# A four-mixer block on one core of Trainium2: nine places in the order of work, and GpSimd rounding weights

## The chip, the cores and the metric

The kernel runs on one core of a Trainium2 chip. The metric is the device time in microseconds (us) of one execution. The kernel's inputs lie in HBM; all of its work, from loading them to the last store, counts.

## The reference

The reference takes x (512 tokens, width 1024), a context of 256 tokens and a conditioning vector c through a chain of blocks, all in fp32:

```
first block, twice (L0: 512 + 256 context tokens, L1: 512 tokens; L1's context only gives keys and values):
  shift, scale, gate = split(silu(c) @ w_ada + b_ada)            # and the same of c_ctx for the context
  h = rms_norm(x, norm_g) * (1 + scale) + shift
  a_glu, a_gate, nq, nk, nv, n_gate, wq, wk, wv, w_gate, merge = split(h @ w_in)
  y_a = (silu(layer_norm(conv31(a_glu[:512] * sigmoid(a_glu[512:])))) * silu(a_gate)) @ w_proj_a
  y_b = (neighbourhood_attention(rms(nq), rms(nk), nv) * silu(n_gate)) @ w_proj_b    # 8 heads, 8 x 16 window + context, bias
  y_c = (window_attention(rope(rms(wq)), rope(rms(wk)), wv, sink) * silu(w_gate)) @ w_proj_c
  x = x + gate * ((sigmoid(g_a) * y_a + sigmoid(g_b) * y_b + sigmoid(g_c) * y_c) @ w_o)
then x + rglru_mixer(rmsnorm(x)), x + ffn(...), x + nsa_mixer(...), x + ffn(...), and a last norm
rglru_mixer: y, x = split(x @ lru_in);  xc = causal_conv4(x);  r, i = sigmoid(xc @ gate_w);
  log_a = -8 * r * softplus(-a_param);  h = scan(exp(log_a), sqrt(-expm1(2 log_a)) * i * xc);  (h * gelu(y)) @ lru_out
```

## The kernel before

Every product is made of three matmuls of fp32r operands: a weight and an activation are each split into a rounded part (WH; Hh, Gh, XH) and a remainder (WL; Hl, Gl, XL), and hi*hi, hi*lo and lo*hi are added in PSUM. Activations lie with their features on the partitions, so that a chunk of weights, 128 outputs by 1024 inputs (8 blocks of 128 x 128), is used by 24 matmuls over 512 columns, and 24 more over 256 where the context's tokens are there.

**Weights.** All chunks are numbered in the order of their use, W[0], W[1], ... SyncE loads chunk j into one of three buffers RAW (`sp_loads`), once the remainder of chunk j-3 is made. ScalarE rounds it into WH (`act_split`, L1027), when TensorE is through with the chunk three before it. VectorE subtracts for WL (`dve_split`, L1037). TensorE waits for WL (`pe_linear`, L1066, and in the branches L1585). `ahead(name)` is the chunk two after the named one: while TensorE works on one, the split of the one two later is issued. For the 32 pieces of the modulation of L1, which are woven into L0, GpSimd subtracts (`pool_split`, L1045). The last entry of a chunk in the plan says how it is split.

**The first block.** `mix(L)` runs the convolution's linears (chunks cb and ca in turn), the neighbourhood branch (br 0), the window branch (br 1) and w_o. Each branch's order of work is one list, written by `branch(L, br)`, and each engine's program walks through that list and issues its own part of each unit. A unit ("lin", name, k, ...) is block k of a chunk, three products for all columns. Phase ph has the chunks of ak, aq, av (keys, queries, values) of head pair ph and ag, mg (gates) of the pair before it. `chain` says at which linear after a chunk's begin its norm is made (nrm1, nrm2, nrm3: squares, sums over the head through TensorE, the scaling); "out" are the copies of queries and keys into QA, QB, KA, KB, shared among ScalarE, VectorE (L1985) and GpSimd (L2049); "vt" and "vout" turn the values and copy them to V (L1905). `heads(p)` gives the units of head pair p, woven between the linears of the phase after it: "st" are scores, with their exponentials Pa and Pb by ScalarE (L1787), "pv" products with V (L1708), "max" the score tiles whose maxima VectorE takes for the next head (L1655, L1661 on TensorE, L1996 on VectorE), "tr" their transposes (L1625), "fin" and "sink" the end. An integer in that list is a linear before which the next unit may not stand: 2 at the start, 22 (19 in br 1) for the next head's maxima.

`taps` are the 31 taps of the depthwise convolution, VectorE's multiply-adds (L1455), two in a unit. In L0 one unit stands after every third linear of the phases and after every second one of the branch's tail; in L1 after every fifth and every second.

The tail of br 0 has the chunks mg (1024 wide) and pj (512 wide) in turn, then cg, cm and pa. `beside` puts one tick of the modulation (a chunk of w_ada times c, L1398) after each of 32 blocks of L0's tail, and behind each eight of them a "modend", which turns the row of results into columns (L1250). A third of w_ada for L1 (part c = 3) is used at the transition from L0 to L1, in `mix(1)`, eight ticks ahead of the norm of L1.

**The recurrent mixer.** After its norm, `recur(m)` runs for ten m in a software pipeline: chunk rx of lru_in, a causal convolution of four taps (L2382, L2386), remainder (L2389), chunk gw of gate_w (256 wide), the gates. Then ten chunks ry with the scans (L2416). The splits are ScalarE's and VectorE's, as everywhere; GpSimd has nothing to do.

## Time and profile before

| | |
|---|---|
| time, median of 3 runs | 3355.71 us (3349.92 to 3362.6) |
| the profiled execution, its time | 3353.82 us |
| its span in the profile | 3352.0 us |
| mean granted clock of TensorE | 0.967 |
| busy: TensorE, VectorE, ScalarE, GpSimd | 93%, 55%, 39%, 8% |
| from HBM | 247 MB, 74 GB/s over the span |

The profile is one execution. Busy time of TensorE counts its matmuls, whose ends are modelled; the granted clock is the share of its full clock (2.4 GHz; the lower level is 1.2 GHz), and a mean between the two is a mix in time. "Waits" sum the idle time ahead of an instruction by the instruction that ended it; "issue" there is idle time whose end no shown semaphore explains. Several waits of one instruction are put down to the one that came last. L1708 is line 1708 of the kernel.

### The profile page before, as it was taken

How to read it: one execution, taken by the hardware profiler on the slowest of the kernel's cores; microseconds unless marked ns; L12 is line 12 of the kernel's file. 1: busy time of each engine (PE TensorE's matmuls, PEld its weight loads, DVE VectorE, ACT ScalarE, POOL GpSimd, SP SyncE). 2: the span in 40 equal slices, each digit the busy share in tenths (PEclk: the TensorE clock that was granted, in tenths of full speed). 3: DMA queues.
4: the chain of work that ended last, by engine and by line, in shares of the span. 5: the costliest groups of instructions: out<-in, count | busy, mean ns of one | idle time of the engine just before them, and what ended most of it. 6: DMA issues, size and time to landing. Idle time of an engine off the chain costs nothing.

```text
span 3352.0 us, 36714 instructions
## 1 busy us (share of the span) xinstructions
PE 3124.0 (93%) x14684; PEld 2439.8 (73%) x14684; DVE 1849.6 (55%) x2910; ACT 1319.7 (39%) x2028; POOL 267.8 (8%) x198
## 2 busy tenths in 40 slices
PE   8998889999999889899889998999999989999998
PEld 4876777877788567677667676788877766788876
DVE  5876675454434667674443576566525662366622
ACT  3244434234432344533444356322224556422221
POOL 0011131210000001100000000000002210000000
PEclk9999989999999899999989999999999999999999
DMA  5221122320011322123101222333332210132331
GB/s 199 70 71 57 48 82 90 109 83 26 19 38 59 105 82 82 51 82 102 32 29 44 72 88 73 98 95 94 95 91 88 91 58 1 57 100 89 98 92 61
DMA packets 78729, 251.48 MB, mean 75 GB/s; under 512 B 9120, under 2 KB 11168, under 8 KB 78560
## 3 DMA queue, kind: packets, MB, share of 16 engines
q1 hardware_dynamic: 72672, 227.91, 22.1%
q0 software_dynamic: 5024, 18.09, 1.7%
q8 instruction: 116, 1.90, 0.2%
q10 hardware_dynamic: 864, 3.15, 0.2%
q14 instruction: 53, 0.43, 0.0%
HBM read 247.01 MB, written 2.10 MB: 74 GB/s over the span
## 4 chain that ended last, share of the span: by engine, by line
PE 41%; DVE 6%; ACT 5%; issue 1%; DMA 0%; DVEq 0%; ACTq 0%; SPq 0%
PE PS L1066 29%; PE PS L1585 2%; PE PS L2521 2%; PE PS L2622 1%; PE PS L1708 1%; PE PS L1090 1%; ACT WH L1027 1%; PE PS L2599 1%; DVE U L2386 1%; PE PS L2600 1%; DVE WL L1037 0%; PE PS L2581 0%; PE PS L2543 0%; DVE IG L2416 0%; ACT PS L2675 0%
## 5 line engine op out<-in xcount | busy, mean ns | idle before, releaser
L1037 DVE TENSOR_TENSOR WL<-RAW,WH 128x1024 fp32r<-128x1024 f32 (+3 forms) x386 | 451.7, 1171 | 581.5 <-ACT WH L1027 580.6
L1027 ACT ACTIVATE WH<-RAW 128x1024 fp32r<-128x1024 f32 (+4 forms) x439 | 422.7, 967 | 475.6 <-PE PS L1066 362.5
L1585 PE MATMUL PS<-Hh,WH 128*128 128x512 f32 x1376 | 533.8, 388 | 12.1 <-DVE T L1956 7.1
L1585 PE MATMUL PS<-Hl,WH 128*128 128x512 f32 x1376 | 496.3, 361 | 0.0
L1585 PE MATMUL PS<-Hh,WL 128*128 128x512 f32 x1376 | 494.6, 359 | 0.0
L1066 PE MATMUL PS<-XH,WH 128*128 128x512 f32 x928 | 372.6, 401 | 23.1 <-DVE WL L1037 16.1
L1066 PE MATMUL PS<-XL,WH 128*128 128x512 f32 x928 | 369.3, 398 | 0.0
L1066 PE MATMUL PS<-XH,WL 128*128 128x512 f32 x928 | 369.0, 398 | 0.0
L1585 PEld LDWEIGHTS PS<-Hh,WH 128*128 128x128 f32 x1376 | 267.7, 195 | 77.7 <-issue 24.6
L1585 PEld LDWEIGHTS PS<-Hl,WH 128*128 128x128 f32 x1376 | 267.5, 194 | 49.7 <-issue 11.2
L1585 PEld LDWEIGHTS PS<-Hh,WL 128*128 128x128 f32 x1376 | 266.5, 194 | 40.3
L1455 DVE SCALAR_TENSOR_TENSOR C<-AP,SMA,C 128x512 f32<-128x512 f32 x360 | 235.1, 710 | 0.4
L1066 PEld LDWEIGHTS PS<-XH,WH 128*128 128x128 f32 x928 | 175.7, 189 | 73.1 <-ACT U L2308 11.9
L1066 PEld LDWEIGHTS PS<-XH,WL 128*128 128x128 f32 x928 | 175.7, 189 | 43.3
L1066 PEld LDWEIGHTS PS<-XL,WH 128*128 128x128 f32 x928 | 175.8, 189 | 43.0 <-issue 1.0
L1045 POOL TENSOR_TENSOR WL<-RAW,WH 128x1024 fp32r<-128x1024 f32 (+1 forms) x53 | 121.8, 2299 | 1028.3 <-ACT WH L1027 1028.3
L1066 PE MATMUL PS<-FGh,WH 128*128 128x512 f32 x384 | 156.5, 408 | 0.0
L1066 PE MATMUL PS<-Hh,WH 128*128 128x512 f32 (+1 forms) x384 | 144.8, 377 | 12.2 <-DVE WL L1037 6.9
L1066 PE MATMUL PS<-FGh,WL 128*128 128x512 f32 x384 | 151.7, 395 | 0.0
L1066 PE MATMUL PS<-FGl,WH 128*128 128x512 f32 x384 | 151.6, 395 | 0.0
L1066 PE MATMUL PS<-Hl,WH 128*128 128x512 f32 (+1 forms) x384 | 139.5, 363 | 0.0
L1066 PE MATMUL PS<-Hh,WL 128*128 128x512 f32 (+1 forms) x384 | 139.0, 362 | 0.0
(375 smaller groups left out, 5434.3 us busy)
## 6 DMA issues: line engine op xcount, KB each, us to landing
RAW<-in_w_in SPq DMA_DIRECT2D x124, 512.0 KB, 3.6
RAW<-in_ffn_in SPq DMA_DIRECT2D x96, 512.0 KB, 3.6
RAW<-in_ffn_out SPq DMA_DIRECT2D x48, 512.0 KB, 3.5
RAW<-in_w_ada SPq DMA_DIRECT2D x32, 384.0 KB, 3.6
RAW<-in_nsa_in SPq DMA_DIRECT2D x21, 512.0 KB, 3.3
RAW<-in_lru_in SPq DMA_DIRECT2D x20, 512.0 KB, 3.6
MW<-in_w_ada SPq DMA_DIRECT2D x32, 256.0 KB, 9.1
BS<-in_bs POOLq DMA_DIRECT2D x16, 512.0 KB, 3.9
```

The costliest lines, as they stand in the source:

```text
L1027: act.activation(WH[half[j]][:, 0:n], RAW[j % NRAW][:, 0:n], ACT.Copy).then_inc(*did("act_whi", ("whi", j)))
L1037: dve.tensor_tensor(WL[half[j]][:, 0:n], RAW[j % NRAW][:, 0:n], WH[half[j]][:, 0:n].bitcast(F32), ALU.subtract).then_inc(*did("dve_wlo", ( ...
L1045: pool.tensor_tensor(WL[half[j]][:, 0:n], RAW[j % NRAW][:, 0:n], WH[half[j]][:, 0:n].bitcast(F32), ALU.subtract).then_inc(*did("pool_wlo", ...
L1066: mm = pe.matmul(ps[:, c:c + n], wt[:, 128 * i:128 * i + 128], x[:, a:a + n], start=(seen == 0 and q == 0), stop=(seen == total - 1 and q ...
L1090: pe.matmul(ps[:, c:c + n], ones, b[:, a0:a0 + n], start=(k == 0), stop=(k == 7)).then_inc(*did("pe_sq", ("sqm", sq, k)))
L1455: dve.scalar_tensor_tensor(dst, src, wt, dst, ALU.mult, ALU.add).then_inc(*did("dve_tap", ("tap", L, m, k, a0), ("tap", L, m, k)))
L1585: mm = pe.matmul(ps[:, c:c + w_], wt[:, 128 * k:128 * k + 128], x[:, a:a + w_], start=(k == 0 and q == 0), stop=(k == n - 1 and q == 2))
L1708: mm = pe.matmul(dst, VV[L, br][:, b, 64 * g:64 * g + 128], src, start=first, stop=end)
L2386: dve.scalar_tensor_tensor(xc, pa[:, k:k + S], smc(cw + 4 * m + k, cw + 4 * m + k + 1), xc, ALU.mult, ALU.add).then_inc(*did("dve_c", *([( ...
L2521: mm = pe.matmul(ps[:, 0:S], wt[half[j]][:, 128 * k:128 * k + 128], x[:, k, :], start=(k == 0 and q == 0), stop=(k == 7 and q == 2))
L2599: pe.matmul(ps3, NKH[b][:, g, 128 * kt:128 * kt + 128], by_tile(NQ[:, 4 * g:4 * g + 4, :], qt), start=True, stop=False)
L2600: mm = pe.matmul(ps3, NKL[b][:, g, 128 * kt:128 * kt + 128], by_tile(Q2[g % 2], qt), start=False, stop=kt < qt)
```

## The change

The weights' splits in the attention branches are issued at unit k = 3 of a chunk instead of k = 0 by ScalarE and VectorE. A fourth way to split, POOLED, lets GpSimd both round and subtract; it is used for the chunks ak, aq, av, ag and the first mg of L1's window branch and for lru_in and gate_w. GpSimd's copies of QB and KA in L1's window branch go to ScalarE. Norms' second part moves from linear 10 to 11, third part in br 0 from 13 to 14. In br 0 head pairs start at linear 4, the next maxima at 27 (L0) or 25 (L1), and the first half of the copies at 24. Taps begin later in each phase but the first, and come every 1.8 linears in the tails. The modulation's ticks stand two blocks later and modend one block more; at the transition two of the eight ticks and the order of chunks move behind the first linear. The first norm's split of weights stands after row 2 instead of 5.

```diff
+POOLED = 4
@@ mix(L)
-            for k in range(8):
+            for k in range(4):
                 self.tick(3, k)
@@ conv(L)
             self.win(("cb", L, m), L, 512 + 128 * m)
+            if (L, m) == (1, 0):
+                for k in range(4, 8):
+                    self.tick(3, k)
@@ chain
-            c = {8: [("nrm1", nm)], 10: [("nrm2", nm)], 13: [("nrm3", nm)]}
+            c = {8: [("nrm1", nm)], 11: [("nrm2", nm)], 13 if br else 14: [("nrm3", nm)]}
@@ heads
-            start = [5] + tops(0, 0) + a + rows(0, 0) + b if p == 0 else [2]
-            ready = 19 if br else 22
+            start = [5] + tops(0, 0) + a + rows(0, 0) + b if p == 0 else [2 if br else 4]
+            ready = 19 if br else 27 if L == 0 else 25
@@ tapped
-        def tapped(units, every):
-            out, n = [], 0
+        def tapped(units, every, late=False):
+            out, n = [], -every if late else 0
...
-                    if n % every == 0 and taps:
+                    if n > 0 and int(n / every) > int((n - 1) / every) and taps:
@@ phases
-                    at.setdefault(1 if f else 18 if br else 22, []).extend(to)
+                    at.setdefault(1 if f else 18 if br else 24, []).extend(to)
-            order += tapped(made, 3 if L == 0 else 5) + ...
+            order += tapped(made, 3 if L == 0 else 5, ph > 0) + ...
-        ticks = iter(range(32 if L == 0 and not br else 0))
+        spots = iter(range(-2, 30))
         def beside(steps):
...
+            out = list(steps)
+            if L == 0 and not br and (i := next(spots)) >= 0:
+                out += tick(i)
+            return out
+        def tick(i):
+            return ([("modend", L, i // 8 - 2)] if i % 8 == 1 and i > 8 else []) + [("tick", i // 8 - 1, i % 8)]
-        order += tapped(tail, 2) + taps
+        order += tapped(tail, 1.8) + taps
-        return order + ([("modend", L, 2)] if L == 0 else [])
+        return order + (tick(30) + tick(31) + [("modend", L, 2)] if L == 0 else [])
@@ attn
+                    woven = nm[0] in ("ak", "aq", "av", "ag") or nm[0] == "mg" and nm[3] < 3 + br
+                    self.linear(nm, [((u[3], u[4], 0, 128 * u[5], POOLED if woven and L and br else 1), list(range(u[5])))])
@@ recur, lru
+        self.linear(nm, [(("lru_in", 10 + m, 0, 1024, POOLED), list(range(8)))])
+        self.chunk(("gw", m), 0, ("gate_w", m, 0, 256, POOLED))
+            self.linear(nm, [(("lru_in", m, 0, 1024, POOLED), list(range(8)))])
@@ act_split
-                if how:
+                if how and how != POOLED:
+        def pool_weights(pool, upto):
+            while done["pool"] <= min(upto, len(P.W) - 1):
+                j = done["pool"]
+                n, how = P.W[j][3:5]
+                if how == POOLED:
+                    for w in due("pool", ("raw", j), earlier[j], ("turn", done["turn"])):
+                        pool.wait_ge(*w)
+                    pool.tensor_copy(WH[half[j]][:, 0:n], RAW[j % NRAW][:, 0:n]).then_inc(*did("pool_whi", ("whi", j)))
+                    pool_split(pool, [j])
+                done["pool"] += 1
@@ act_begin (dve_begin alike)
-            act_rms(act, "in", HH[0], ..., (5, 1))
+            act_rms(act, "in", HH[0], ..., (2, 1))
@@ pe_conv
+                if (L, m) == (1, 0):
+                    for k in (6, 7):
+                        pe_tick(pe, 3, k)
@@ act_attn (dve_attn alike)
-                    if u[2] == 0:
+                    if u[2] == 3:
                         act_split(act, ahead(nm))
@@ act_out
+            if L and br:
+                if kind == "ak":
+                    to = to if f == 0 else [(KA[L, br][64:128, 1, 0:n], 64, "p1")] + to
+                else:
+                    to = to + [(QB[L, br][0:64, 0, 0:n], 0, "p0")] if f == 0 else [(QB[L, br][64:128, 1, 0:n], 64, "p1")] + to
@@ pool_attn
+            pool_weights(pool, P.wj[("ak", L, br, 0), 0] + 1)
...
-                if u[0] == "out":
+                if u[0] == "lin":
+                    if u[2] == 0:
+                        pool_weights(pool, ahead(nm))
+                elif u[0] == "out" and not (L and br):
@@ pe_mix
-                for k in range(1, 8):
+                for k in range(1, 6):
                     pe_tick(pe, 3, k)
@@ act_mix (dve_mix alike, with dve_split)
                 act_rms(act, sq, HH[L], ..., (1, P.wj[("cb", 1, 0), 0] + 1))
+                act_split(act, P.wj[("ca", 1, 0), 0])
@@ pool program
             pool_mix(pool, 1)
+            pool_weights(pool, P.wj[("ry", 9), 0])
             pool_nsa(pool)
```

## Rows read from the trace of the kernel before

**Rows 1.** Page, part 1: busy time, share of the span and instructions by engine.

```profile
...
PE 3124.0 (93%) x14684; PEld 2439.8 (73%) x14684; DVE 1849.6 (55%) x2910; ACT 1319.7 (39%) x2028; POOL 267.8 (8%) x198
...
```

**Rows 2.** Waits of PE: line <- releaser: us in total, times, longest us.

```profile
...
PE PS L1066 <- DVE WL L1037: 23.0, 11, 4.8
...
PE PS L1708 <- ACT Pa L1787: 18.2, 14, 3.0
...
PE PS L1708 <- DVE V L1905: 13.2, 6, 4.1
PE PS L1655 <- DVE QA L1985: 12.5, 4, 5.1
...
PE PS L1655 <- issue: 9.5, 4, 2.4
...
PE PS L1398 <- POOL WL L1045: 6.8, 1, 6.8
...
PE PS L1250 <- ACT T L1263: 6.0, 2, 4.8
...
```

**Rows 3.** Busy by stretch: PE, PEld, DVE, ACT, POOL (count), granted clock, DMA share.

```profile
...
223.00:295.00 72.00, 60.25 (x309) 49.60 (x307) 49.31 (x78) 29.51 (x45) 10.79 (x11) 0.93 0.20 59
430.00:470.00 40.00, 33.20 (x157) 26.89 (x158) 28.55 (x43) 12.03 (x15) 17.55 (x4) 0.81 0.30 92
1420.00:1465.00 45.00, 38.45 (x148) 29.33 (x149) 43.03 (x61) 15.05 (x20) 0.73 (x1) 0.92 0.20 54
1932.00:1990.00 58.00, 53.99 (x216) 41.91 (x216) 45.63 (x77) 27.87 (x46) 0.00 (x0) 0.94 0.25 75
1990.00:2067.00 77.00, 61.49 (x246) 47.95 (x246) 59.78 (x77) 61.03 (x81) 0.00 (x0) 0.96 0.25 73
...
```

**Rows 4.** Timeline, PE, two linears in a row at full clock: first product of each.

```profile
...
450.05 0.39 PE L1585 MATMUL PS<-Hh,WH 128*128 128x512 f32 x1
...
451.10 0.39 PE L1585 MATMUL PS<-Hh,WH 128*128 128x512 f32 x1
...
```

**Rows 5.** Timeline, PE, three stretches: start, us, instruction, idle before and its end.

```profile
...
49.77 0.80 PE L1066 MATMUL PS<-Hh,WH 128*128 128x512 f32 x1 [3.62 <-DVE WL L1037]
...
299.07 2.05 PE L1708 MATMUL PS<-Pa,V 128*128 128x512 f32 x2 [4.06 <-DVE V L1905]
...
1114.84 0.80 PE L1066 MATMUL PS<-Hh,WH 128*128 128x512 f32 x1 [3.25 <-DVE WL L1037]
...
```

**Rows 6.** Timeline, DVE, two stretches: before a copy of V, and beside POOL's splits.

```profile
...
296.78 1.15 DVE L1455 SCALAR_TENSOR_TENSOR C<-AP,SMA,C 128x512 f32<-128x512 f32 x2
...
458.25 2.58 DVE L1037 TENSOR_TENSOR WL<-RAW,WH 128x1024 fp32r<-128x1024 f32 x1 [6.79 <-ACT WH L1027]
460.76 4.37 DVE L1455 SCALAR_TENSOR_TENSOR C<-AP,SMA,C 128x512 f32<-128x512 f32 x4
...
```

**Rows 7.** Timeline, DVE, one group of the recurrent mixer (rx and gw).

```profile
...
1942.62 1.22 DVE L1037 TENSOR_TENSOR WL<-RAW,WH 128x1024 fp32r<-128x1024 f32 x1
...
1948.30 0.42 DVE L1037 TENSOR_TENSOR WL<-RAW,WH 128x256 fp32r<-128x256 f32 x1
...
1950.16 1.22 DVE L1037 TENSOR_TENSOR WL<-RAW,WH 128x1024 fp32r<-128x1024 f32 x1
```

**Rows 8.** Timeline, POOL, two stretches: its first splits and two later ones.

```profile
...
432.98 12.75 POOL L1045 TENSOR_TENSOR WL<-RAW,WH 128x1024 fp32r<-128x1024 f32 x2 [6.11 <-ACT WH L1027]
...
457.35 2.40 POOL L1045 TENSOR_TENSOR WL<-RAW,WH 128x1024 fp32r<-128x1024 f32 x1 [11.62 <-ACT WH L1027]
461.79 2.40 POOL L1045 TENSOR_TENSOR WL<-RAW,WH 128x1024 fp32r<-128x1024 f32 x1 [2.04 <-ACT WH L1027]
```

**Rows 9.** Timeline, ACT, L1's window attention: a split ahead of copies and exponential.

```profile
...
1771.07 1.06 ACT L1027 ACTIVATE WH<-RAW 128x1024 fp32r<-128x1024 f32 x1
...
```

**Rows 10.** Groups of POOL's instructions by line and shape, whole span.

```profile
...
L2049 POOL CAST QB<-T 64x768 fp32r<-64x768 f32 x16 | 17.1, 1066 | 175.0 <-DVE T L1974 136.7 <-DVE T L1964 37.5 <-POOL O L2067 0.5
...
L2485 POOL CAST Q<-NQ 64x2048 fp32r<-64x2048 f32 x3 | 5.7, 1898 | 72.1 <-PE PS L2622 72.1
...
```

More of the change, by code:

```diff
@@ L459, in branch @@
                 elif to and (ph > 1 or f == 0):
-                    at.setdefault(1 if f else 18 if br else 22, []).extend(to)
+                    at.setdefault(1 if f else 18 if br else 24, []).extend(to)
             made, late = woven(steps, at, 0, n, heads(ph - 1))
-            order += tapped(made, 3 if L == 0 else 5) + ([("gate", L, br, ph - 1, f) for f in range(2)] if ph else [])
+            order += tapped(made, 3 if L == 0 else 5, ph > 0) + ([("gate", L, br, ph - 1, f) for f in range(2)] if ph else [])
         assert not late
         order += [("split", ("ag", L, br, m)) for m in range(4)]
-        ticks = iter(range(32 if L == 0 and not br else 0))
+        spots = iter(range(-2, 30))
         def beside(steps):
-            out = steps[0:3]
-            if (i := next(ticks, None)) is not None:
-                if i and i % 8 == 0:
-                    out += [("modend", L, i // 8 - 2)]
-                steps = steps + [("tick", i // 8 - 1, i % 8)]
-            return out + steps[3:]
+            out = list(steps)
[4 more added lines that the diff above has]
+            return ([("modend", L, i // 8 - 2)] if i % 8 == 1 and i > 8 else []) + [("tick", i // 8 - 1, i % 8)]
         def merge(m):
@@ L520, in attn @@
                 if u[2] == 0:
-                    self.linear(nm, [((u[3], u[4], 0, 128 * u[5], 1), list(range(u[5])))])
+                    woven = nm[0] in ("ak", "aq", "av", "ag") or nm[0] == "mg" and nm[3] < 3 + br
+                    self.linear(nm, [((u[3], u[4], 0, 128 * u[5], POOLED if woven and L and br else 1), list(range(u[5])))])
             elif kind == "nrm1":
@@ L637, in recur @@
         nm = ("rx", m)
-        self.linear(nm, [(("lru_in", 10 + m, 0, 1024, 1), list(range(8)))])
+        self.linear(nm, [(("lru_in", 10 + m, 0, 1024, POOLED), list(range(8)))])
         self.tmp.take((nm, "pa"))
@@ L664, in lru @@
             nm = ("ry", m)
-            self.linear(nm, [(("lru_in", m, 0, 1024, 1), list(range(8)))])
+            self.linear(nm, [(("lru_in", m, 0, 1024, POOLED), list(range(8)))])
             if m in (0, 1, 3, 5, 7):
@@ L1336, in dve_begin @@
             dve_turn0(dve, 1)
-            dve_rms(dve, "in", HH[0], HL[0], [("roots",)] + [("x", i) for i in range(6)], lambda k, q: AB[:, k, q:q + 1], lambda k, q: MODS[0][:, k, q:q + 1], (5, 1))
+            dve_rms(dve, "in", HH[0], HL[0], [("roots",)] + [("x", i) for i in range(6)], lambda k, q: AB[:, k, q:q + 1], lambda k, q: MODS[0][:, k, q:q + 1], (2, 1))
         B1 = MODS[0][:, 8:16, 0]
@@ L2045, in pool_attn @@
                     for dst, at, key in to:
-                        for w in due("pool", (nm, "y2") if br else (nm, "y"), scores_read(L, br, p - 1, f), ("pool", L, br, turn)):
+                        for w in due("pool", (nm, "y2") if br else (nm, "y"), scores_read(L, br, p - 1, f), ("turn", done["turn"])):
                             pool.wait_ge(*w)
-                        turn += 1
-                        pool.tensor_copy(dst, y[at:at + 64, 0:n]).then_inc(*did("pool_st", (nm, key), (nm, "out", f), ("pool", L, br, turn)))
+                        done["turn"] += 1
+                        pool.tensor_copy(dst, y[at:at + 64, 0:n]).then_inc(*did("pool_st", (nm, key), (nm, "out", f), ("turn", done["turn"])))
                 elif u[0] == "tick":
```

24 lines of the change are left out of this document (12 added, 12 removed).

## The prediction

> **What bounds the kernel now.** The page comes first. TensorE is busy for 3124.0 us, 93% of the span of 3352.0 [rows 1]. So there are some 228 us in which it stands, plus what it loses at its lower clock, and nothing else can be won: no matmul is removed. VectorE (55%), ScalarE (39%) and GpSimd (8%) have room on average, but that says nothing of one stretch. The list of TensorE's waits is the second view, since the change is a list of stops: it names the instruction that waited, who released it, and how often [rows 2]. The stretches are the third. In 1420:1465, the tail of L1's neighbourhood branch, VectorE is busy 43.03 of 45 us and bounds the work; in the recurrent mixer (1932:1990 and 1990:2067) it is busy 79% and 78%; elsewhere it has air [rows 3]. The granted clock there is the third thing to see. With levels of 1.2 and 2.4 GHz a mean of 0.93 over 72 us means 10.1 us at the lower one, and TensorE, busy 0.84 of the time, lost 10.1 x 0.84 / 2 = 4.2 us. A linear (three products, 768 columns) takes 1.05 us at the full clock, a chunk eight of them, 8.4 us [rows 4].
>
> The sum is made against the profiled execution, 3353.8 us, 1.9 below the median of the runs, 3355.7. A run can tell a change from none at about 0.5%, 17 us.
>
> **Neighbourhood branches: heads, pins, values, copies, splits at k = 3.** The stops for QA (12.5 us, 4 times) and for V (13.2 us, 6 times) [rows 2] are waits for VectorE's copies while TensorE's next instruction is a score or a product of the other head. The longest for V, 4.06 us, is typical [rows 5]: two taps, 1.15 us, ran at 296.78 [rows 6] while TensorE stood. The heads of later phases start two linears later, the maxima wait until unit 27 instead of 22, and the split of 1.22 us [rows 7] no longer stands in front of the copies at a chunk's start. Two linears later is 2.1 us more for each wait, and the split gone is 1.2: 3.3 us against mean waits of 3.1 and 2.2. I take 20 of 25.7 us. The second rotation of norms later by one linear helps one wait and hurts the next: nothing, with 0 to +6 as bounds, as its copies are now later by the same 1.05. Of the low clock behind these stops I take 5 us (a bit over one such stretch of 4.2 us, of some four). Bounds for the part: -8 and -36. Sum -25.
>
> **The first tick of the modulation.** TensorE stood 6.8 us for GpSimd's remainder [rows 2]. That split and the next took 12.75 us together, while a later one took 2.40 [rows 8], so the first took about 10.3. Whether this was VectorE's queue of taps or the first use, no row says. With the tick two blocks later, TensorE has a chunk more of linears; if the 10.3 us come again, 1 to 2 us of waiting are left. The stretch 430:470 is granted 0.81, thus 15.2 us low, 6.3 us lost over two stops [rows 3]; I take 2.5. Sum -7.3, bounds -9.5 and -2.
>
> **Ends of the modulation one block later.** They cost 6.0 us in two waits for ACT's T [rows 2], and the clock behind, some 2. The block inserted takes more than the longest wait, 4.8. Against it two PSUM pairs of the modulation stay taken for one block, so linears have two of four: +1.5. Sum -6.5, bounds -8 and +3.
>
> **Start and transition.** The first linear waited 3.62 us for WL at 49.77, the transition's 3.25 us at 1114.84 [rows 5]. The split at k = 2 costs rows 3 to 7 of the norm about 2.1 us, and these have slack until the linear reaches them: -3. At the transition the raw chunk arrives earlier, since ticks 6 and 7 stand behind it; they still cost their own time: -2. Bounds of both: -7 and +3.
>
> **Splits off ScalarE's way.** TensorE waited 18.2 us for Pa in 14 places and 9.5 us in four places where a copy of QA by ScalarE stood last ("issue") [rows 2]. In L1's window attention ScalarE does a split of 1.06 us right before these copies and exponentials [rows 9], and L0's are alike. Moving it to k = 3 or to GpSimd could take 1.06 from each of 18 waits, 19 us; a wait of mean 1.3 us is often shorter than that, and half of the time something else is next. L1's second branch pays one more copy of about 0.6 us on ScalarE per half. Sum -9, bounds -19 and 0.
>
> **L1's tail.** VectorE bounds it, and it gets 26 taps instead of 22, and its splits later in the chunk, where TensorE needs them sooner. A tap is 0.58 to 0.74 us (1.15 for two) [rows 6]: 4 x 0.73 = 2.9, and about as much for late remainders: +6, bounds +2 and +9. In L0's tail VectorE is busy 28.55 of 40 us [rows 3], which covers four more taps.
>
> **GpSimd splits the recurrent mixer.** No row shows GpSimd rounding a 128x1024 chunk. Its casts of 64x768 take 1.07 us and of 64x2048 1.90 us [rows 10], so about 1.2 for 1024; with the subtraction of 2.40 [rows 8] a chunk costs 3.6 us, a chunk of 256 about 1.3, against 1.22 and 0.42 on VectorE [rows 7]. The price lies in the two engines together: VectorE's remainder that began at 458.25 lasted 2.58 instead of 1.22 us and ended 1.08 us after GpSimd's subtraction, which ran 457.35 to 459.75; the four taps at 460.76 lasted 4.37 instead of 2.3, with GpSimd's at 461.79 inside [rows 6, 8]. So I count their work there as one queue. The group rx and gw takes 7.54 us now, from 1942.62 to 1950.16 [rows 7], and VectorE is busy 0.79 of it [rows 3], 5.93; without 1.22 and 0.42 that is 4.29. With GpSimd's 4.9 it is 9.2 us, 1.65 more per group, 16.5 over ten. For the ten ry chunks VectorE has 59.78 - 12.2 = 47.6 us, GpSimd 36: 83.6 against a stretch of 77 [rows 3]: +6.6. Sum +23. The ends: without any such lock all waits of L1066 for WL but the two priced above go (23.0 - 3.6 - 3.3 = 16.1 us) and some 4 us of clock, -20; with delays inside VectorE's chain of dependent instructions, and with GpSimd's first chunks running against the norm ahead, +38.
>
> The Trainium skill ("SBUF — State Buffer", section "Who interferes with whom") says that the pair of ports that the two engines share is an exclusive lock for a whole instruction, and that a VectorE instruction with at most one SBUF input is free of it; of the group's instructions the two tensor-scalar ones (about 1.05 us, by the length of two taps) would then be outside, the group 8.15 us, and the mixer's price some +12 instead of +23. The trace agrees with the lock in the two places above; that a one-input instruction escapes it, no row of mine shows.
>
> **GpSimd splits L1's window attention.** VectorE is idle for most of this stretch, so it meets GpSimd less: +2 for longer copies, bounds -3 and +10.
>
> **Sum:** -25 - 7.3 - 6.5 - 5 - 9 + 6 + 23 + 2 = -21.8. That is 3332 for the profiled execution and 3334 against the median.
>
> **Rivals.**
> A, the forecast, 3334 us, chance 0.42; its own spread is 15 us each way, so that it can fall within 0.5%.
> B, the two engines hardly disturb each other in the mixer. For it: the subtraction itself stays at 2.40 us beside busy taps [rows 8], and GpSimd does nothing at all in the mixer now [rows 3]. Against it: the 2.58 us. The mixer gives -20, the time is 3334 - 43 = 3291. Chance 0.20.
> C, the stops move. The matmuls stay as many, and a wait taken from V or QA comes back at the next product, for Pa, Pb or a transpose, because the heads' chain of scores, exponentials and products is itself what is late. For it: Pa already is the wait with the most places, 14 [rows 2]. Against it: the longest waits end with a copy that stood behind other work. Then some 33 of the 53 us won outside the mixer are kept, and mixer, tail and window attention cost 31: 3355.7 - 2 = 3354. Chance 0.21.
> D, slower: one mechanism, the mixer's weights on GpSimd. If its two instructions for a chunk take 5 us instead of 3.6 because they wait for VectorE's as well, VectorE's 4.3 and GpSimd's 7 stand in one line and the group takes 11 us, 3.5 more; ten groups cost 35 and the ry chunks 15. With 8 for the tail and window attention and 33 won elsewhere that is 3355.7 + 25 = 3381. It decides from about 10.5 us per group on, where the mixer eats all that the rest gains (30 + 15 = 45 = 53 - 8). For it: the first split of 10.3 us beside VectorE's taps [rows 8]. Against it: the later ones at 2.40. Chance 0.17.
>
> **How the numbers follow.** Faster by over 0.5% is below 3338.9: most of B, six tenths of A, a tenth of C: 0.19 + 0.25 + 0.02, and a little for sizes that I took low: 0.49. Slower, above 3372.5: most of D and a little of C: 0.19. The rest, 0.32, is within 0.5%. The range from 3290 to 3373 leaves out a third of B and two thirds of D. That is A's own 3319 to 3349 widened by B and C.
>
> **What would show it.** In the changed trace: no wait of TensorE over 1.5 us for V and QA in L0's neighbourhood branch, and a clock of 0.96 or more there; the first tick's wait under 2 us; none over 1 us for ACT's T at the modulation's ends. GpSimd's subtraction at 2.40 us but its rounding spread widely; VectorE's three-operand instructions in the mixer at mean over 1.0 us instead of about 0.75; the spacing of rx chunks 9 us instead of 7.54; TensorE's clock falling there. In L1's tail 6 us more. The prediction is wrong in its main point if the mixer's groups keep 7.5 us or less, or if the waits for V and QA come back under other names with the same total.

## The result: 0.8% slower, and the profile after

The changed kernel takes 3385.1 us (median of four runs, 3380.5 to 5035.7) against 3355.5 for the one before (four runs, 3349.9 to 3362.6): ratio 1.0083, interval 1.0057 to 1.0108. In a later comparison five runs of it took 3380.0 to 3381.6 us, and the ratio is 1.0067 (1.0053 to 1.0080). The run of 5035.7 us had a mean granted clock of 0.554 and is left out of the ratio; the profile shown here is of another execution of the same kernel, 3378.2 us in span. The first view is the page, as in [rows 1].

```profile
span 3378.2 us, 36730 instructions
...
PE 3121.0 (92%) x14684; PEld 2438.2 (72%) x14684; DVE 1866.2 (55%) x2866; ACT 1290.6 (38%) x1993; POOL 403.0 (12%) x277
...
```

TensorE does the same 14684 matmuls and is busy as long as before; it stands some 29 us more. GpSimd's busy time went from 267.8 to 403.0 us. VectorE's rose from 1849.6 to 1866.2 although it makes 44 remainders fewer, some 46 us of work: its other instructions became longer. What TensorE waits for, in the columns of [rows 2] (L1608 is the old L1585, L1086 the old L1066, L1731 the old L1708, L1678 the old L1655, L1648 the old L1625, L1653 the old L1630, L1270 the old L1250):

```profile
...
PE PS L1608 <- DVE T L1984: 20.4, 8, 3.3
PE PS L1086 <- ACT U L2341: 20.1, 3, 10.7
PE PS L1731 <- ACT Pa L1810: 17.6, 15, 4.1
PE PS L1653 <- DVE T L1992: 17.0, 6, 4.0
PE PS L1678 <- DVE QA L2013: 16.8, 5, 6.9
...
PE PS L1086 <- DVE XL L1161: 13.4, 4, 12.6
PE PS L1608 <- DVE WL L1045: 12.9, 7, 4.1
PE PS L1678 <- issue: 11.6, 4, 5.0
...
PE PS L1648 <- ACT T L1833: 9.2, 6, 1.9
...
PE PS L1270 <- ACT T L1283: 2.1, 1, 2.1
...
```

The 13.2 us for V are gone, those for ACT's T of the transposes (L1648) fell from 19.8 to 9.2, and the first tick's 6.8 us are gone. In their place stand the waits for T of the norms, 20.4 and 17.0 us (7.1 and 3.2 before, at the old L1585 and L1630), and those of the mixer, for ACT's U and for XL. QA was 12.5 us in four places and is 16.8 in five. In L0's neighbourhood phases alone (120 to 431 us) no wait of TensorE for V or QA is left under its name, where there were 9.5 and 10.1 us; but T of the norms went from 2.4 to 10.4 us, "issue" ahead of the score tiles from nothing to 9.9, and TensorE's waits there add up to about 41 us, as before. Then the stretches, as in [rows 3]:

```profile
...
430.00:470.00 40.00, 38.36 (x211) 31.85 (x211) 39.20 (x58) 10.49 (x13) 15.18 (x4) 0.99 0.41 117
1930.00:1990.00 60.00, 52.53 (x220) 40.58 (x219) 51.65 (x55) 15.00 (x25) 39.38 (x30) 1.00 0.25 71
1990.00:2020.00 30.00, 17.69 (x61) 13.36 (x60) 24.21 (x29) 14.20 (x22) 13.00 (x9) 0.77 0.29 87
...
```

The first tick's stretch (430:470), 0.81 before, is now granted 0.99 and TensorE is busy 38.36 of 40 us in it. The mixer's clock falls to 0.77 in 1990:2020, behind two stops of 6 us.

The traces were laid side by side by the start of the same matmul in both (the one of each chunk's first 512 columns with WL), which gives how much longer each stage became. The second column is the changed kernel, the third the same with the mixer's weights back on ScalarE and VectorE (e1_lru_back), the fourth that one with the branches' splits back at unit 0 (f3_split_k0); us against before, of one execution each:

| stage | changed | mixer back | and splits at 0 | forecast |
|---|---|---|---|---|
| start and L0's convolution | -4.2 | -4.1 | -3.5 | -3 |
| L0, neighbourhood phases | -0.1 | +2.0 | -13.1 | most of -25 |
| first tick | -10.3 | -10.3 | -10.6 | -7.3 |
| rest of L0's tail | +11.5 | +11.5 | +7.8 | -6.5 |
| L0, window attention | +9.6 | +9.7 | +5.5 | most of -9 |
| w_o and transition | -2.3 | -2.4 | -3.5 | -2 |
| L1, neighbourhood phases | +8.4 | +8.4 | -0.6 | rest of -25 |
| L1's tail | +5.3 | +5.3 | +5.2 | +6 |
| L1, window attention | -18.5 | -18.5 | -14.0 | +2 |
| mixer | +27.5 | +0.3 | +0.3 | +23 |

Behind the mixer none of the experiments below changes anything, and still the profiled executions of all these kernels lie there between 1.2 us below and 5.8 us above that of the kernel before. A single stage of a single execution is thus no firmer than a few us.

### The profile page after: what moved, and what is told of

Its sections match the earlier page's. It is cut to its first block, busy times and chain, and to the rows that moved or that the text cites. A ratio compares the mean times of both kernels' runs of the same rounds, so it can differ in the third digit from the quotient of the medians.

```text
span 5033.8 us, 36730 instructions
## 1 busy us (share of the span) xinstructions
PE 4957.0 (98%) x14684; PEld 2993.4 (59%) x14684; DVE 1872.7 (37%) x2866; ACT 1299.6 (26%) x1993; POOL 386.7 (8%) x277
## 4 chain that ended last, share of the span: by engine, by line
PE 52%; DVE 1%; ACT 1%; issue 0%; DMA 0%; ACTq 0%; DVEq 0%; SPq 0%
PE PS L1086 35%; PE PS L2554 4%; PE PS L1608 4%; PE PS L2655 1%; PE PS L1110 1%; PE PS L1731 1%; PE PS L2632 1%; PE PS L2614 1%; PE PS L2633 1%; PE PS L2615 1%; PE PS L2576 0%; PE PS L2323 0%; PE PS L1741 0%; PE PS L2648 0%; PE PS L2637 0%; PE PS L1711 0%
## 5 line engine op out<-in xcount | busy, mean ns | idle before, releaser
L1608 PE MATMUL PS<-Hh,WH 128*128 128x512 f32 x1376 | 743.6, 540 | 1.0 <-DVE WL L1045 0.6
L1045 DVE TENSOR_TENSOR WL<-RAW,WH 128x1024 fp32r<-128x1024 f32 (+2 forms) x342 | 396.9, 1161 | 833.5 <-ACT WH L1035 832.4
L1608 PE MATMUL PS<-Hh,WL 128*128 128x512 f32 x1376 | 696.2, 506 | 0.0
L1608 PE MATMUL PS<-Hl,WH 128*128 128x512 f32 x1376 | 696.1, 506 | 0.0
L1035 ACT ACTIVATE WH<-RAW 128x1024 fp32r<-128x1024 f32 (+3 forms) x395 | 383.7, 974 | 853.8 <-PE PS L1086 658.7
L1086 PE MATMUL PS<-XH,WH 128*128 128x512 f32 x928 | 537.8, 580 | 12.2 <-DVE XL L1161 12.2
L1086 PE MATMUL PS<-XL,WH 128*128 128x512 f32 x928 | 535.2, 577 | 0.0
L1086 PE MATMUL PS<-XH,WL 128*128 128x512 f32 x928 | 534.9, 576 | 0.0
L1608 PEld LDWEIGHTS PS<-Hh,WH 128*128 128x128 f32 x1376 | 314.8, 229 | 179.7 <-issue 115.1
L1608 PEld LDWEIGHTS PS<-Hl,WH 128*128 128x128 f32 x1376 | 320.2, 233 | 159.0 <-issue 101.2
L1608 PEld LDWEIGHTS PS<-Hh,WL 128*128 128x128 f32 x1376 | 311.1, 226 | 126.0 <-issue 51.2
L1054 POOL TENSOR_TENSOR WL<-RAW,WH 128x1024 fp32r<-128x1024 f32 (+2 forms) x97 | 211.1, 2176 | 1309.6 <-ACT WH L1035 1306.1
L1086 PEld LDWEIGHTS PS<-XH,WH 128*128 128x128 f32 x928 | 202.8, 219 | 169.8 <-issue 104.6
L1086 PEld LDWEIGHTS PS<-XL,WH 128*128 128x128 f32 x928 | 203.5, 219 | 154.6 <-issue 92.7
L1086 PEld LDWEIGHTS PS<-XH,WL 128*128 128x128 f32 x928 | 203.4, 219 | 152.8 <-issue 89.1
L1086 PE MATMUL PS<-FGh,WH 128*128 128x512 f32 x384 | 229.9, 599 | 0.0
L1086 PE MATMUL PS<-FGh,WL 128*128 128x512 f32 x384 | 221.3, 576 | 0.0
L1086 PE MATMUL PS<-FGl,WH 128*128 128x512 f32 x384 | 220.9, 575 | 0.0
L1086 PE MATMUL PS<-Hh,WH 128*128 128x512 f32 (+1 forms) x384 | 203.3, 529 | 2.4 <-DVE Hl L1163 2.4
L1086 PE MATMUL PS<-Hh,WL 128*128 128x512 f32 (+1 forms) x384 | 197.0, 513 | 0.0
L1086 PE MATMUL PS<-Hl,WH 128*128 128x512 f32 (+1 forms) x384 | 196.2, 511 | 0.0
```

The costliest lines, as they stand in the source:

```text
L1035: act.activation(WH[half[j]][:, 0:n], RAW[j % NRAW][:, 0:n], ACT.Copy).then_inc(*did("act_whi", ("whi", j)))
L1045: dve.tensor_tensor(WL[half[j]][:, 0:n], RAW[j % NRAW][:, 0:n], WH[half[j]][:, 0:n].bitcast(F32), ALU.subtract).then_inc(*did("dve_wlo", ( ...
L1054: pool.tensor_tensor(WL[half[j]][:, 0:n], RAW[j % NRAW][:, 0:n], WH[half[j]][:, 0:n].bitcast(F32), ALU.subtract).then_inc(*did("pool_wlo", ...
L1086: mm = pe.matmul(ps[:, c:c + n], wt[:, 128 * i:128 * i + 128], x[:, a:a + n], start=(seen == 0 and q == 0), stop=(seen == total - 1 and q ...
L1608: mm = pe.matmul(ps[:, c:c + w_], wt[:, 128 * k:128 * k + 128], x[:, a:a + w_], start=(k == 0 and q == 0), stop=(k == n - 1 and q == 2))
```

## Experiments

Medians in us, with the difference from the kernel before, which ran on the same chip beside each group (e, f, g, h: 3358.2, 3356.1, 3357.1, 3357.1 us), and the ratio to it with its 95% interval. The four groups ran on four chips, so kernels of different groups are compared by the third column: what an edit wins or costs is the difference of two of its entries. The expectations compare bare medians, which gives up to 2 us more or less.

| kernel | median | against before | ratio, interval |
|---|---|---|---|
| changed (e0_after) | 3380.4 | +22.2 | 1.0067, 1.0053 to 1.0080 |
| mixer's weights back (e1_lru_back) | 3358.1 | -0.1 | 0.9998, 0.9989 to 1.0007 |
| window attention's back (e2_wa_back) | 3400.0 | +41.8 | 1.0124, 1.0110 to 1.0138 |
| both back (e3_both_back) | 3373.5 | +15.3 | 1.0047, 1.0034 to 1.0060 |
| e1 and norms as before (f1_norms_back) | 3363.0 | +7.0 | 1.0020, 1.0010 to 1.0031 |
| e1 and heads as before (f2_heads_back) | 3360.7 | +4.7 | 1.0014, 1.0005 to 1.0024 |
| e1 and splits at unit 0 (f3_split_k0) | 3330.1 | -26.0 | 0.9923, 0.9908 to 0.9938 |
| e1 and taps as before (f4_taps_back) | 3349.7 | -6.4 | 0.9984, 0.9975 to 0.9994 |
| f3 and taps as before (g1_k0_taps) | 3331.2 | -26.0 | 0.9931, 0.9914 to 0.9947 |
| f3 and norms as before (g2_k0_norms) | 3325.5 | -31.6 | 0.9908, 0.9893 to 0.9922 |
| f3 and heads as before (g3_k0_heads) | 3338.2 | -18.9 | 0.9947, 0.9932 to 0.9962 |
| f3 and window attention's weights back (g4_k0_wa) | 3344.3 | -12.9 | 0.9963, 0.9950 to 0.9976 |
| e1, only ScalarE's split at unit 0 (h2_act0) | 3329.3 | -27.8 | 0.9917, 0.9902 to 0.9931 |
| g2, the ry chunks on GpSimd (h3_ry_pool) | 3333.6 | -23.5 | 0.9930, 0.9915 to 0.9945 |
| g2, first copies at 22 (h4_out22) | 3320.1 | -37.0 | 0.9890, 0.9875 to 0.9905 |
| h4, L1's taps every second linear (h5_out22_taps) | 3312.6 | -44.5 | 0.9866, 0.9850 to 0.9883 |

**The changed kernel as it is.**

> The changed kernel as it is, for a profile at the full clock and a time beside the next three. Both theories: 3380 to 3386 us. Theory one (the mixer): the recurrent mixer, from its norm to its last ry chunk, is 40 us or more longer than before and the rest of the kernel 10 to 25 us shorter. Theory two (the places): the mixer is at most 15 us longer and the rest 15 us or more longer, its stops having moved.

The time fits both theories, and the stages fit neither: the mixer is 27.5 us longer, between the 40 of the one and the 15 of the other, and the rest is neither shorter nor longer.

**The mixer's weights back.**

```diff
-        self.linear(nm, [(("lru_in", 10 + m, 0, 1024, POOLED), list(range(8)))])
+        self.linear(nm, [(("lru_in", 10 + m, 0, 1024, 1), list(range(8)))])
...
```

> The changed kernel with lru_in's and gate_w's chunks split by ScalarE and VectorE again, all else as changed. Theory one (the mixer's weights on GpSimd cost 40 to 60 us): 3330 to 3345 us, faster than the kernel before. Theory two (the price lies in the moved places or the window attention): 3370 us or more. My forecast's own price for this edit, 23 us, would give 3362.

It wins 22.3 us, the price that the forecast had. It ends at the time of the kernel before, outside both theories (3330 to 3345, and 3370 or more) and nearest to the forecast's own price, 3362. Everything else together was worth nothing.

**The window attention's weights back, and both.**

```diff
-                    self.linear(nm, [((u[3], u[4], 0, 128 * u[5], POOLED if woven and L and br else 1), list(range(u[5])))])
+                    self.linear(nm, [((u[3], u[4], 0, 128 * u[5], 1), list(range(u[5])))])
```

> The changed kernel with the weights of L1's window attention split by ScalarE and VectorE again (at unit 3 of a chunk), the copies of QB and KA still ScalarE's, the mixer still GpSimd's. Theory one: within 6 us of the changed kernel, 3379 to 3391. Theory three (the window attention's weights on GpSimd are what costs, their 3.6 us a chunk being too long for a chunk of 5.6 us with the copies between): 3360 us or less.

> Both edits undone: no weights rounded by GpSimd at all. Theory one: as with the mixer's alone undone, 3325 to 3345 us, so the moved places by themselves win 10 to 30 us. Theory two: 3365 us or more, the moved places lose by themselves.

No theory had this: without GpSimd's splits in the window attention the kernel is 19.6 us slower (15.4 between e1 and e3), and in the trace the difference lies in that stage: -18.4 us against before in e0, +1.5 in e2. What is left without any rounding by GpSimd, the moved places alone, loses 15 us, as theory two had it.

**One place at a time, from e1.**

```diff
# f1: norms
-            c = {8: [("nrm1", nm)], 11: [("nrm2", nm)], 13 if br else 14: [("nrm3", nm)]}
+            c = {8: [("nrm1", nm)], 10: [("nrm2", nm)], 13: [("nrm3", nm)]}
# f2: heads, pins, copies
-            start = [5] + tops(0, 0) + a + rows(0, 0) + b if p == 0 else [2 if br else 4]
-            ready = 19 if br else 27 if L == 0 else 25
+            start = [5] + tops(0, 0) + a + rows(0, 0) + b if p == 0 else [2]
+            ready = 19 if br else 22
-                    at.setdefault(1 if f else 18 if br else 24, []).extend(to)
+                    at.setdefault(1 if f else 18 if br else 22, []).extend(to)
# f3: splits, in ScalarE's and in VectorE's program
-                    if u[2] == 3:
+                    if u[2] == 0:
# f4: taps
-            order += tapped(made, 3 if L == 0 else 5, ph > 0) + ...
-        order += tapped(tail, 1.8) + taps
+            order += tapped(made, 3 if L == 0 else 5) + ...
+        order += tapped(tail, 2) + taps
```

> From the changed kernel with the mixer's weights back on ScalarE and VectorE (3358 us): the norms' second part at linear 10 again instead of 11, and the third at 13 in both branches. Theory P (the later norms cost, since the chunk after waits for the PSUM pair that the third part reads, and the rotation waits for the third part): the waits for T at L1984 and L1992, 20.4 and 17.0 us, fall to about 7 and 3, the waits for T at L1833 rise by about 10, and the time is 3335 to 3348 us. Rival Q (the places are neutral one by one, a chain of exponentials and products is what is late): 3352 us or more, the waits only change their names.

> From the same kernel: heads of later phases of the neighbourhood branch start at linear 2 again, next maxima at 22, first copies at 22. Theory P: the heads' later start won the V stops but lengthened the stops for QA; taking it back brings V's 13 us back and takes as much from QA and Pb: 3350 to 3366 us, no clear change. My forecast's view (the later heads win 20 us): 3375 us or more. A view in which they lose by themselves: 3345 us or less.

> From the same kernel: ScalarE and VectorE split the weights of the attention branches at unit 0 of a chunk again instead of unit 3. Theory P (splits at unit 3 fall onto the norm's work, which now comes one linear later): 3345 to 3355 us, mostly in L1's tail (some 3 us) and in the T waits. My forecast's view (unit 3 frees copies and exponentials, worth up to 19 us): 3365 us or more.

> From the same kernel: taps as before (no late start in the phases, one unit after every second linear of the tails, 22 instead of 26 units in L1's tail). Theory P: L1's tail wins back 3 to 5 us of its 5.3, L0's phases lose less than that: 3352 to 3358 us. Rival (late taps are what makes room for copies of QA and V): 3362 us or more.

The splits at unit 3 cost 25.9 us, more than any view had. Norms: theory P fell, the later ones win 7 us here. Heads: 4.7 us won, as P had it; the intervals of e1 and f2 overlap. By stage the later heads win 8.0 us in L0's phases and lose 8.6 in L1's. Taps: 6.3 us lost, a little more than P had. So the late split is the largest single part of what the forecast missed. The trace shows how. Unit 3 of a chunk is linear 11 counted from the begin of the chunk before, and there the norm's second part stands. Three timelines of the changed kernel (start, us, engine, line, operation, idle before): ScalarE, VectorE, and the linear of TensorE that waits:

```profile
...
247.75 1.05 ACT L1839 ACTIVATE T<-PS,EPSC 128x384 f32<-128x384 f32 x2 [2.54 <-PE PS L1648]
248.69 0.94 ACT L1843 ACTIVATE T<-T 128x384 f32<-128x384 f32 x2
249.52 1.05 ACT L1035 ACTIVATE WH<-RAW 128x1024 fp32r<-128x1024 f32 x1
...
```

```profile
...
250.60 1.23 DVE L1045 TENSOR_TENSOR WL<-RAW,WH 128x1024 fp32r<-128x1024 f32 x1 [1.76 <-ACT WH L1035]
251.75 1.14 DVE L1478 SCALAR_TENSOR_TENSOR C<-AP,SMA,C 128x512 f32<-128x512 f32 x2
252.81 0.68 DVE L2031 TENSOR_REDUCE STAT<-PS 128x2 f32<-128x512 f32 x1
253.52 0.97 DVE L2045 TENSOR_TENSOR PS<-PS,O 64x768 f32<-64x768 f32 x1
...
256.40 1.01 DVE L1980 SCALAR_TENSOR_TENSOR T<-T 128x384 f32<-128x384 f32 x2
257.33 1.01 DVE L1984 SCALAR_TENSOR_TENSOR T<-PS,T 128x384 f32<-128x384 f32 x2
...
```

```profile
...
258.40 0.50 PE L1608 MATMUL PS<-Hh,WH 128*128 128x512 f32 x1 [3.34 <-DVE T L1984]
...
```

ScalarE makes the norm's logarithms and exponentials (to 249.6) and then rounds the weight, to 250.57. VectorE's queue has the subtraction at the same place, so it stands 1.76 us idle for WH, then subtracts. Only then come two taps, a reduction and the three instructions that end a head, none of which needs the weight, and the norm's third part at 256.40, 6.8 us after the exponentials. The linear at 258.40 waits for that part's second step (L1984), because it needs the PSUM pair that the step reads: 3.34 us. In the kernel with splits at unit 0 the same stretch, VectorE and then ScalarE:

```profile
...
238.06 1.23 DVE L1045 TENSOR_TENSOR WL<-RAW,WH 128x1024 fp32r<-128x1024 f32 x1 [1.61 <-ACT WH L1035]
...
245.25 0.97 DVE L2045 TENSOR_TENSOR PS<-PS,O 64x768 f32<-64x768 f32 x1 [0.43 <-ACT O L1894]
...
248.13 1.01 DVE L1980 SCALAR_TENSOR_TENSOR T<-T 128x384 f32<-128x384 f32 x2
...
```

```profile
...
236.98 1.05 ACT L1035 ACTIVATE WH<-RAW 128x1024 fp32r<-128x1024 f32 x1
...
242.57 0.94 ACT L1843 ACTIVATE T<-T 128x384 f32<-128x384 f32 x2
...
```

Rounding and subtraction are over at 239.3, ahead of the norm's logarithms. The exponentials end at 243.5 and the third part starts at 248.13, 4.6 us later instead of 6.8. TensorE's waits in that kernel, whole span, in the same columns:

```profile
...
PE PS L1731 <- ACT Pa L1810: 22.0, 14, 4.1
...
PE PS L1648 <- ACT T L1833: 11.1, 8, 2.3
...
PE PS L1608 <- DVE T L1984: 7.0, 5, 2.2
...
PE PS L1653 <- DVE T L1992: 7.0, 6, 2.8
...
```

T of the norms fell from 20.4 to 7.0 and from 17.0 to 7.0.

**Which engine's late split.**

```diff
# ScalarE's program only
-                    if u[2] == 3:
+                    if u[2] == 0:
                         act_split(act, ahead(nm))
```

> From the changed kernel with the mixer's weights back (3358 us): in the attention branches ScalarE rounds at unit 0 again, VectorE subtracts at unit 3. If VectorE's wait for WH in front of the norm's third part is what the late split costs (its idle time, 1.8 us, at 250.6 in the trace), most of the 28 us come back: 3332 to 3340 us. If VectorE's own 1.2 us at that place, and WL coming late, are what costs: 3346 to 3356 us.

All of it comes back, 27.7 us, with VectorE's subtraction still at unit 3. The same stretch of this kernel, ScalarE and then VectorE:

```profile
...
235.36 1.05 ACT L1035 ACTIVATE WH<-RAW 128x1024 fp32r<-128x1024 f32 x1
...
240.95 0.94 ACT L1843 ACTIVATE T<-T 128x384 f32<-128x384 f32 x2
...
```

```profile
...
240.97 1.22 DVE L1045 TENSOR_TENSOR WL<-RAW,WH 128x1024 fp32r<-128x1024 f32 x1
...
246.76 1.01 DVE L1980 SCALAR_TENSOR_TENSOR T<-T 128x384 f32<-128x384 f32 x2
...
```

The subtraction stands in the same place, but its WH has been ready for 4.5 us, so VectorE doesn't stop. The norm's third part begins 4.9 us after the exponentials, instead of 6.8. TensorE's waits for T of the norms are 7.2 and 7.0 us, as in f3 (7.0 and 7.0; 20.4 and 17.0 in e1), and VectorE's own idle time for WH in L0's phases is 5.1 us instead of 34.8. So it is ScalarE's late place that cost, and these rows show it through VectorE's wait; the reverse, ScalarE late and VectorE early, was not run, so what the 1.05 us cost ScalarE's own work is not known by itself. VectorE's late place is not free either: TensorE's waits for WL in the branches are 16.4 us in ten places, against 9.2 in six in f3, but the two kernels' times don't differ beyond their intervals.

**The same places again, from f3.**

> From the kernel with the mixer's weights back on ScalarE and VectorE and the branches' splits back at unit 0 (3330 us): taps as before too. If the tails' 26 units are what L1's tail still pays, 3320 to 3326 us, with the waits for WL in L1's tail (9.2 us) down to about 4. If the late taps were hiding the copies only now that the splits are early, 3330 or more.

> From the same kernel (3330 us): norms at 10 and 13 again. Theory P2 (a split at the same unit as the norm's second part was the whole trouble, so with early splits the later norms help): 3333 to 3345 us, waits for T at L1833 up from 11 to about 20. Theory P3 (later norms cost by themselves, a PSUM pair held longer and the rotation late): 3318 to 3326 us.

> From the same kernel (3330 us): heads, pins and first copies of the neighbourhood branch as before (2, 22, 22). If the later heads win by themselves as forecast, but were covered by the late splits: 3338 to 3352 us with V's stops of 13 us back. If they only exchange V's stops for QA's: 3326 to 3334 us.

> From the same kernel (3330 us): the window attention's weights of L1 back on ScalarE and VectorE, at unit 0. If GpSimd's part is worth the 15 to 20 us that the changed kernel loses without it whatever the unit of the split: 3345 to 3352 us. If most of that was only the late split of the rival arrangement, it is worth 3 to 8 us: 3333 to 3338 us. My forecast had it at a loss of 2: 3328 us.

The edits are those of f4, f1, f2 and e2. With early splits the taps are neutral (0.0 us), where they cost 6.3 beside late ones; in the traces of f3 and g1 two effects stand behind that zero: the late start in the phases wins 5.0 us in L0 and 3.5 in L1, the closer taps of the tails lose 0.7 and 5.2. Later norms cost 5.6 us, where they won 7: their sign hangs on the split. P3 holds, if barely: the intervals of f3 and g2 overlap by 0.0014. The later heads win 7.1 us, at the lower edge of the expectation in which they win, so the forecast had their direction and not their size; by stage they win 13.1 us in L0's phases and lose 4.6 in L1's. GpSimd's splits in the window attention win 13.1 us here too, again in that stage (-14.0 us against -0.5). TensorE's waits there for ScalarE's Pa and Pb, for the maxima and for QA are 13.9 us in f3 and 24.3 in g4.

**The mixer in two parts.**

```diff
# from g2
-            self.linear(nm, [(("lru_in", m, 0, 1024, 1), list(range(8)))])
+            self.linear(nm, [(("lru_in", m, 0, 1024, POOLED), list(range(8)))])
```

> From the best kernel so far (3325 us, early splits, norms as before, mixer's weights on ScalarE and VectorE): only the ten ry chunks of the mixer on GpSimd. My forecast's sum for these, 6.6 us, gives 3332. If the 24 us of the whole mixer come mostly from the first part (norm, rx, gw): 3325 to 3333. If from the scans with their chain of dependent instructions on VectorE: 3336 to 3346 us.

8.1 us for the ten ry chunks, where the sum had 6.6; some 14 of the 22.3 us remain for the norm, rx and gw, where it had 16.5. In the profiled executions the mixer's stage is 12.9 us longer than in g2, while the stages behind it, which the edit doesn't touch, are 4.2 shorter, so that 8.1 is rather too low.

**Copies, and L1's taps.**

```diff
# h4, from g2
-                    at.setdefault(1 if f else 18 if br else 24, []).extend(to)
+                    at.setdefault(1 if f else 18 if br else 22, []).extend(to)
# h5, from h4
-        order += tapped(tail, 1.8) + taps
+        order += tapped(tail, 1.8 if L == 0 else 2) + taps
```

> From the best kernel so far (3325 us): the first half of the neighbourhood branch's copies at unit 22 again, heads at 4 and next maxima at 27 or 25 as changed. If the stops for QA (13.2 us, and issue) are there because copy and maximum now stand only three units apart: 3310 to 3320 us. If the copies wait for the scores of the head before (they may not overwrite what these read): 3323 to 3328 us.

> From the best kernel so far with the copies at unit 22, and L1's tail with a tap unit at every second linear instead of every 1.8 (L0 as changed). L1's tail pays 5 us in waits for WL in the changed kernel: 3 to 4 us below the kernel with the copies at 22 alone. If four units left to the end of the tail cost the same there: no difference.

The copies two units earlier win 5.4 us, and TensorE's waits for ScalarE's copy of QA, 10.8 us in g2, are gone. Taps at every second linear of L1's tail win 7.5 us between the medians of four runs each. In the profiled executions that tail is 3.6 us shorter and the spans are equal; that execution of h5 is its slowest, 3320.2 us, the other three took 3311.4 to 3312.7. So 7.5 is more than the tail explains, and where the rest lies isn't shown. This is the fastest kernel here, 3312.6 us, 44.5 below the one before and some 67 below the changed one. Its waits:

```profile
...
PE PS L1678 <- DVE STAT L2024: 25.3, 8, 6.1
PE PS L1648 <- ACT T L1833: 22.8, 13, 3.0
...
```

The stops for QA went to STAT (the head's maxima), 25.3 us in eight places, where g2 had 6.8 in six. T of the transposes is at 22.8; it rose from 11.1 to 22.4 with the norms taken back in g2. So stops moved, as rival C has it, down to the last version, and the gain is what is left after it.

## Why the prediction was wrong

The forecast was 3334 us and faster; measured are 3385 and 3380. The range ended at 3373. The step that failed is the late split: the sum counted what it frees at its old place and nothing for its new one (point 2).

1. The mixer, +23: right in its total, 22.3 us by e1 (26.5 between e2 and e3, the same edit with the window attention back on ScalarE and VectorE), and in its mechanism; the parts were off and made up for each other. By the trace's +27.5 the norm ahead costs 6.5 us, which the sum had only in its upper end, rx and gw 12.1 (16.5 in the sum), ry 8.9 (6.6). In the middle of the stretch VectorE's groups follow each other every 8.7 to 8.9 us, where 9.2 was worked out. The mechanism is the one queue of two engines. VectorE's groups in the stretch 1932:1990, the changed kernel and then the one before (columns: line, engine, operation, shapes, count, busy us, mean ns, idle before):

```profile
...
L2419 DVE SCALAR_TENSOR_TENSOR U<-U,SM 128x512 f32<-128x512 f32 x22 | 31.7, 1441 | 0.8
...
L2415 DVE TENSOR_SCALAR U<-U,SM 128x512 f32<-128x512 f32 x7 | 4.2, 600 | 1.0 <-DVE U L2412 0.6
...
```

```profile
...
L2386 DVE SCALAR_TENSOR_TENSOR U<-U,SM 128x512 f32<-128x512 f32 x24 | 18.0, 752 | 0.8
...
L2382 DVE TENSOR_SCALAR U<-U,SM 128x512 f32<-128x512 f32 x8 | 4.4, 547 | 1.3 <-DVE U L2379 0.5 <-ACT U L2322 0.2
...
```

The three-operand instruction with two inputs in SBUF went from 752 to 1441 ns on average, the tensor-scalar with one from 547 to 600. Only two of the seven tensor-scalars ran beside a GpSimd subtraction; they took 0.71 and 0.75 us, a third just behind this stretch 0.55, and all others 0.55. GpSimd's rounding of 1024 columns, which no row had shown, is 1.17 us, and the subtraction 2.60 on average (1.2 and 2.4 in the forecast):

```profile
...
L1054 POOL TENSOR_TENSOR WL<-RAW,WH 128x1024 fp32r<-128x1024 f32 x63 | 163.7, 2599 | 667.0 <-ACT WH L1035 664.2
...
L1063 POOL CAST WH<-RAW 128x1024 fp32r<-128x1024 f32 x34 | 39.8, 1170 | 372.9 <-PE PS L1608 242.9 <-ACT T L1103 92.9 <-PE PS L1086 17.0
...
```

The Trainium skill's rule ("SBUF — State Buffer", "Who interferes with whom") is that a VectorE instruction with at most one SBUF input, outside the modes that use both ports, does not contend with GpSimd. These rows test it weakly: one of three such instructions kept its length and two grew by 0.16 and 0.2 us, far less than those with two inputs. The sum by it, +12, was too low. Both sums left out the norm ahead of the mixer: three chunks are split by GpSimd just when VectorE makes the reciprocal root on which all of it hangs. VectorE, then GpSimd in the changed kernel, then VectorE before:

```profile
...
1904.40 2.12 DVE L1140 SCALAR_TENSOR_TENSOR U<-U 128x256 f32<-128x256 f32 x2 [0.79 <-ACT U L1128]
1906.45 3.73 DVE L1144 TENSOR_TENSOR U<-U 128x256 f32<-128x256 f32 x2
1910.10 2.89 DVE L1148 SCALAR_TENSOR_TENSOR U<-U 128x256 f32<-128x256 f32 x2
...
```

```profile
...
1902.73 2.34 POOL L1054 TENSOR_TENSOR WL<-RAW,WH 128x1024 fp32r<-128x1024 f32 x1
...
1906.33 2.40 POOL L1054 TENSOR_TENSOR WL<-RAW,WH 128x1024 fp32r<-128x1024 f32 x1
...
1909.98 2.40 POOL L1054 TENSOR_TENSOR WL<-RAW,WH 128x1024 fp32r<-128x1024 f32 x1
```

```profile
...
1905.77 0.76 DVE L1124 TENSOR_TENSOR U<-U 128x256 f32<-128x256 f32 x2
...
```

Three steps of 0.76 us, two instructions each, became 2.1, 3.7 and 2.9: 6.5 us more, and TensorE's stop there, for XL, went from 6.1 to 12.6 us.

2. The step that failed: "the split of 1.22 us no longer stands in front of the copies" in the term of the neighbourhood branches (-25), together with the term "Splits off ScalarE's way" (-9). The move of the split was priced as 1.22 or 1.06 us freed at the old place, and never as the same instruction at the new one. Measured, the late split costs 25.9 us, by f3, and by h2 all of it hangs on ScalarE's place: VectorE stands idle there for WH, ahead of the norm's third part, and TensorE waits for that part. The heads' direction was right and their size was not: 7.1 us with early splits, 4.7 with late ones, against 20. The later norms, taken at nothing, cost 5.6 us with early splits and win 7 with late ones. The forecast's own sign of a failure in its main point came: in L0's phases the 19.6 us of waits for V and QA came back under other names with the same total.

3. GpSimd's splits of the window attention were taken at +2 and bring -13 to -20. I had looked at the meeting of the engines, which costs little there, and not at what ScalarE and VectorE no longer do: the forecast's own row of a rounding just ahead of the exponentials [rows 9] belonged to this edit, since it is gone in that stage and only moved in the others. That this is why it wins is read from the waits of f3 and g4; the rounding and the subtraction were not moved one by one.

4. The first tick, -7.3: measured -10.3, of which two ticks' own time, about 1 us each, is only postponed. GpSimd's first subtraction again was long:

```profile
...
433.45 6.79 POOL L1054 TENSOR_TENSOR WL<-RAW,WH 128x1024 fp32r<-128x1024 f32 x1 [10.43 <-ACT WH L1035]
```

6.8 instead of 10.3 us; TensorE no longer waited for it. The modulation's ends, -6.5: the gain came, its price was missed. The waits for ACT's T went from 6.0 to 2.1 us, and the chunk with the longest of them became 7.4 us shorter, but the rest of L0's tail as a whole became 11.5 us longer. TensorE in the changed kernel:

```profile
...
510.77 0.76 PE L1608 MATMUL PS<-Hh,WH 128*128 128x512 f32 x1 [3.29 <-DVE Y L1956]
...
564.49 0.76 PE L1608 MATMUL PS<-Hh,WH 128*128 128x512 f32 x1 [4.10 <-DVE WL L1045]
...
684.56 0.77 PE L1270 MATMUL PS<-CO,T 4*128 4x4 f32 x6 [2.15 <-ACT T L1283]
...
708.84 2.08 PE L1653 MATMUL PS<-T,CO 128*128 128x512 f32 x2 [3.95 <-DVE T L1992]
...
```

A linear at 510.77 waits 3.29 us for VectorE's read of a PSUM pair (Y). The forecast had a shortage of pairs at 1.5, but this stop is 0.7 us with the taps as before (f4), so VectorE's queue has a part in it; it is 5.3 with early splits (f3) and 4.3 with both (g1), so no one edit explains it. One at 564.49 waits 4.1 for WL: this stop is gone in f3 and there in h2, so it is VectorE's late subtraction. At 684.56 the last end waits all the same, with its two ticks, postponed from the first stop, now standing bare: some 4.6 us. The row at 708.84 is the next stage, a rotation that waits for the norm, which the late split delays; in f3 it is 1.4 us. The taps alone make L0's tail 6.0 us longer beside late splits (e1 against f4) and 0.7 beside early ones.

5. Start and transition, -3 and -2: right, -4.2 and -2.3. L1's tail, +6: +5.3, a hit by luck. The sum had 2.9 for four more taps and as much for late remainders; but a unit is two taps, the trace has 58 in that tail instead of 50, and the term is all taps: 4.2 us of it leave with them (f4) and 0.1 with the late splits (f3).

Rival D gave 3381 and one cause, the mixer at +50; the number is near and the cause is not, the mixer cost half of that. What happened is the forecast's own price for the mixer, and C outside of it, in a stronger form: not only did the stops move, a new one was made, VectorE's for ScalarE's late rounding.

## What to carry to other kernels

- A split, copy or any step moved from a queue's place A to B is to be priced at B: what stands behind it there on its engine, what it waits for, and who waits for that. Where all engines walk through one list, a late instruction on one engine can be a wait on another, which holds up instructions of the second that need nothing of it.
- Edits to one order of work aren't additive. The later norms won 7 us with late splits and lost 5.6 with early ones, and the taps cost 6.3 or nothing. Each move wants to be measured by taking it out of the whole, and by stage: the heads' sum of 7 us is a gain in L0 and a loss in L1.
- The same splits on GpSimd won 13 to 20 us in L1's window attention and lost 22 to 27 in the mixer. In the first TensorE waited for exponentials, copies and maxima behind ScalarE's and VectorE's splits; in the second VectorE's chain of two-input instructions, busy 79% of the time, already set the pace.
